# Local attention: doubled value tiles in three passes, another order of a turn, one mask for both halves

## The reference, cut to what matters

```python
# q: 16 heads, k and v: 2 heads of 64; blocks of 128 tokens, a band = the block before and the own block
kb, vb = band(k), band(v)
scores = einsum('bnqhgd,bnkhd->bnhgqk', qb, kb) * scale
diff = (BLOCK + arange(BLOCK))[:, None] - arange(2 * BLOCK)[None, :]
mask = ((diff >= 0) & (diff < WINDOW))[None] & kvalid[:, None, :]      # WINDOW = BLOCK = 128
scores = where(mask, scores, -inf)
probs = softmax(concatenate([scores, sink], -1))[..., :-1]
o = einsum('bnhgqk,bnkhd->bnqhgd', probs, vb)
y_sw = (o * silu(sw_z)) @ w_branch_swa
```

## Time and profile before

| | |
|---|---|
| median of 3 executions | 978.87 us (978.41 to 978.96) |
| profiled execution | 977.73 us |
| its span, first to last instruction | 975.9 us |
| mean granted PE clock | 0.998 |
| PE / DVE / ACT / POOL busy | 949.2 / 638.8 / 479.5 / 273.9 us |
| local attention, from PE's first score to the first product of slab 21 | 718.81 to 811.74 us |

### The profile page before, as it was taken

The page is one execution under the profiler, slowest core; times in us unless marked ns, Lnnn a source line. Parts: engine busy times, 40 slices in busy tenths (PEclk is TensorE's granted clock), DMA queues, the critical chain, the costliest instruction groups (busy, mean ns, idle before and its releaser), DMA issues.

```text
span 975.9 us, 12816 instructions
## 1 busy us (share of the span) xinstructions
PE 949.2 (97%) x4766; PEld 794.2 (81%) x4766; DVE 638.8 (65%) x921; ACT 479.5 (49%) x881; POOL 273.9 (28%) x208
## 2 busy tenths in 40 slices
PE   7999999999999999999999999998999889999997
PEld 6988888888888888888888888887887667888886
DVE  5677777937787687846666798699557775312214
ACT  5444655624435655725347777433556662222222
POOL 2216200003126200002342010430337996224231
PEclk9999999999999999999999999999999999999999
DMA  9332201232422301133233011131320112323312
GB/s 295 107 121 67 86 22 44 65 113 86 142 87 87 108 23 44 44 130 83 87 119 98 1 44 44 44 129 49 116 75 1 43 44 84 111 89 105 130 44 86
DMA packets 64990, 80.37 MB, mean 82 GB/s; under 512 B 5520, under 2 KB 48656, under 8 KB 64928
## 3 DMA queue, kind: packets, MB, share of 16 engines
q1 hardware_dynamic: 63024, 76.64, 24.5%
q10 hardware_dynamic: 1904, 2.88, 0.9%
HBM read 77.42 MB, written 2.10 MB: 81 GB/s over the span
## 4 chain that ended last, share of the span: by engine, by line
PE 43%; issue 31%; DVE 10%; POOL 9%; ACT 6%; DMA 1%; POOLq 0%; ACTq 0%; DVEq 0%
PE ps L1992 12%; PE ps L1993 11%; PE ps L1994 11%; POOL pwt L706 3%; PE ps L2051 1%; PE ps L2049 1%; PE ps L2050 1%; POOL yw L683 1%; POOL qw L691 1%; DVE rot L1848 1%; DVE wlo L1649 1%; DVE sp L1743 1%; ACT spr L1008 1%; POOL wlo L698 1%; DVE yw L1910 1%
## 5 line engine op out<-in xcount | busy, mean ns | idle before, releaser
L633 POOL TENSOR_TENSOR wlo<-raw,whi 128x2048 fp32r<-128x2048 f32 (+1 forms) x22 | 96.5, 4387 | 185.3 <-ACT whi L1002 175.9
L1992 PE MATMUL ps<-whi,hhi 128*128 128x512 f32 (+1 forms) x320 | 115.7, 362 | 1.1 <-issue 0.3
L1992 PE MATMUL ps<-hhi,whi 128*128 128x512 f32 x288 | 113.7, 395 | 3.3 <-DVE ysb L1286 2.5
L1994 PE MATMUL ps<-whi,hlo 128*128 128x512 f32 (+1 forms) x320 | 114.5, 358 | 0.0
L1993 PE MATMUL ps<-wlo,hhi 128*128 128x512 f32 (+1 forms) x320 | 114.4, 358 | 0.0
L1994 PE MATMUL ps<-hhi,wlo 128*128 128x512 f32 x288 | 112.3, 390 | 0.0
L1993 PE MATMUL ps<-hlo,whi 128*128 128x512 f32 x288 | 112.2, 390 | 0.0
L1002 ACT ACTIVATE whi<-raw 128x2048 fp32r<-128x2048 f32 (+1 forms) x29 | 52.9, 1826 | 81.7 <-PE ps L1994 73.2
L1320 DVE TENSOR_TENSOR wlo<-raw,whi 128x2048 fp32r<-128x2048 f32 (+1 forms) x29 | 63.6, 2192 | 37.4 <-ACT whi L769 30.9
L769 ACT ACTIVATE whi<-raw 128x2048 fp32r<-128x2048 f32 (+1 forms) x29 | 52.1, 1797 | 69.3 <-PE ps L1994 69.3
L2049 PE MATMUL ps<-hhi,whi 128*128 128x512 f32 x192 | 76.8, 400 | 0.0
(11 more groups left out here) (337 smaller groups left out, 2293.3 us busy)
## 6 DMA issues: line engine op xcount, KB each, us to landing
raw<-in_w_in SPq DMA_DIRECT2D x42, 1024.0 KB, 5.3
raw<-in_w_out SPq DMA_DIRECT2D x12, 1024.0 KB, 5.0
raw<-in_w_in SPq DMA_DIRECT2D x10, 512.0 KB, 3.9
raw<-in_w_branch_swa SPq DMA_DIRECT2D x4, 1024.0 KB, 5.0
raw<-in_w_branch_sb SPq DMA_DIRECT2D x4, 512.0 KB, 3.4
x<-in_x ACTq DMA_DIRECT2D x3, 512.0 KB, 6.7
out<-x SPq DMA_DIRECT2D x3, 512.0 KB, 2.6
ws<-in_spatial_w SPq DMA_DIRECT2D x2, 512.0 KB, 6.5
```

Of the source, the lines that this page charges most:

```text
L633: pool.tensor_tensor(wlo[s][:, 0:n, :], raw[s][:, 0:n, :], whi[s][:, 0:n, :].bitcast(F32), ALU.subtract).then_inc(slab_split, 1)
L1992: pe.matmul(out_ap, lhsT=lhi(k), rhs=rhi(k), start=first and k == 0, stop=False, skip_group_check=True)
L1994: m = pe.matmul(out_ap, lhsT=llo(k), rhs=rhi(k), start=False, stop=last and k == n - 1, skip_group_check=True)
```

## The change

- The value tiles are doubled instead of halved: `before_hi`, `before_lo`, `step_hi`, `step_lo` hold each half of a value twice (64 + 64 columns), so a product puts the same sum into both halves of the partitions. `window_values` runs three passes for the earlier values and three for the differences: six products instead of four. The 0.5 that stood in the tiles moves to the output.
- ACT makes the high halves of the differences ahead of the second half of the q tokens, and those of the earlier values after the last gate columns. POOL makes all low halves, and `v_step` itself behind slab 12's low half instead of slab 10's. DVE makes none.
- `other_half` and `window_gated` go. DVE's `window_out` takes PSUM times 0.5 times the gate at once.
- `window_own_low` goes. DVE masks both halves in one instruction, after a wait for its own split.
- Order of a turn: PE transposes turn w ahead of the values of turn w - 1, and the two gate steps of turn 0 come ahead of its transposes. DVE, ACT and POOL make a turn's maximum, exponentials, reciprocal and scaling one turn earlier; the outputs follow one turn after their products instead of two or three.
- Slab 18's low half goes from DVE to POOL, behind the first two scalings. Slab pieces keep their turns, counted from a loop shifted by one.

```diff
-                if j == 10:
+                if j == 12:
                     pool.wait_ge(tokw_copied, 3)
...
+            def values_low(lo, v, hi, copy_):
+                return pool.tensor_tensor(lo[:, :, :, copy_, :], v.rearrange("p t (g d) -> p t g d", g=2),
+                                          hi[:, :, :, copy_, :].bitcast(F32), ALU.subtract)
+            pool.wait_ge(vw_hi, 1)
+            for copy_ in range(2):
+                values_low(step_lo, v_step[:], step_hi, copy_).then_inc(vw_lo, 1)
+            pool.wait_ge(vw_hi, 2)
+            pool.wait_ge(tw_done, 10)
+            for copy_ in range(2):
+                values_low(before_lo[:, 0:1], insert_dim(v_meta[:], 1, 1), before_hi[:, 0:1], copy_)
+                values_low(before_lo[:, 1:], tokw[:, 0:3, 1152:1280], before_hi[:, 1:], copy_).then_inc(vw_lo, 1)
...
+            window_normalised(0)
+            window_normalised(1)
+            split2_lo(18)
             for w in range(16):
                 if w:
-                    window_own_low(w - 1)
-                if w >= 2:
-                    window_gated(w - 2)
-                if w >= 3:
-                    window_out_lo(w - 3)
+                    window_out_lo(w - 1)
+                if w < 14:
+                    window_normalised(w + 2)
...
+            def values_high(hi, v):
+                for copy_ in range(2):
+                    last = copy(hi[:, :, :, copy_, :], v.rearrange("p t (g d) -> p t g d", g=2))
+                return last
             for half in range(2):
                 split2(11 + 2 * half)
-                if half == 0:
+                if half == 1:
                     act.wait_ge(v_step_ready, 2)
+                    values_high(step_hi, v_step[:]).then_inc(vw_hi, 1)
...
             act.wait_ge(rope2_done, 5)
+            act.wait_ge(vw_lo, 2)
+            values_high(before_hi[:, 0:1], insert_dim(v_meta[:], 1, 1))
+            values_high(before_hi[:, 1:], tokw[:, 0:3, 1152:1280]).then_inc(vw_hi, 1)
...
+            merge_tanh(0)
+            for w in range(16):
+                transposed_hi(w)
+                if w == 14:
+                    split2(21)
+                if w < 14:
+                    window_exp(w + 2)
...
                 if w:
-                    other_half(w - 1)
+                    window_out_hi(w - 1)
...
                 low(pwt[:, 1, 0, :], ps[:, 4 + w % 2, :], pwt[:, 0, 0, :]).then_inc(tw_lo, 1)
-                dve.tensor_tensor(by_head(pwt[:, 0, 1, :]), by_head(pwt[:, 0, 0, :].bitcast(F32)),
-                                  insert_dim(own_keys.bitcast(F32), 1, 4), ALU.mult).then_inc(window_own_hi, 1)
+                dve.wait_ge(tw_lo, 10 + w + 1)
+                both = lambda own: pwt[:, :, own, :].rearrange("p s (h n) -> p s h n", n=P)
+                dve.tensor_tensor(both(1), both(0).bitcast(F32),
+                                  insert_dim(insert_dim(own_keys.bitcast(F32), 1, 4), 1, 2), ALU.mult).then_inc(window_own, 1)
...
-                    last = dve.tensor_tensor(yw[r, w % 2], o, other_part[r, w % 2], ALU.add)
+                    last = dve.scalar_tensor_tensor(yw[r, w % 2], o, 0.5, gate_sw[r, 2 * u:2 * u + 2, n * P:n * P + P],
+                                                    ALU.mult, ALU.mult)
...
+            window_norm(0)
+            window_norm(1)
+            window_max(2)
+            for w in range(16):
+                if w:
+                    window_out(w - 1)
+                transposed_lo(w)
+                if w == 14:
+                    slab2_low(21)
+                if w < 13:
+                    window_max(w + 3)
+                if w < 14:
+                    window_norm(w + 2)
+            window_out(15)
...
+                pe.wait_ge(tw_hi, 10 + w + 1)
+                pe.wait_ge(vw_lo, 4)
                 if w:
                     pe.wait_ge(swo_read, w)
+                v = lambda tile: tile[:, n, g].rearrange("p a d -> p (a d)")
+                pe.matmul(ps[:, 6, :], lhsT=v(before_hi), rhs=pwt[:, 0, 0, :], start=True, stop=False)
+                pe.matmul(ps[:, 6, :], lhsT=v(before_lo), rhs=pwt[:, 0, 0, :], start=False, stop=False)
+                pe.wait_ge(tw_lo, 10 + w + 1)
+                pe.matmul(ps[:, 6, :], lhsT=v(before_hi), rhs=pwt[:, 1, 0, :], start=False, stop=False)
+                pe.wait_ge(window_own, w + 1)
+                pe.matmul(ps[:, 6, :], lhsT=v(step_hi), rhs=pwt[:, 0, 1, :], start=False, stop=False)
+                pe.matmul(ps[:, 6, :], lhsT=v(step_lo), rhs=pwt[:, 0, 1, :], start=False, stop=False)
+                pe.matmul(ps[:, 6, :], lhsT=v(step_hi), rhs=pwt[:, 1, 1, :], start=False, stop=True).then_inc(swo_done, 1)
...
+                if w < 16:
+                    window_transposed(w)
                 if w:
                     window_values(w - 1)
-                if w < 16:
-                    window_transposed(w)
```

More of the change, by code:

```diff
@@ L700, in part_low, with window_normalised @@
                     ins.then_inc(slab_split, 1)
[L702 to L709, removed]
+            def window_normalised(w):
                 p4 = four_heads(pw, w)[:, :, 0:P]
@@ L1826, in stick_out @@
                 dve.wait_ge(ysb_ready, c + 1)
-            dve.wait_ge(vw_hi, 1)
-            for g in range(2):
-                d = slice(1152 + 64 * g, 1216 + 64 * g)
-                low(vwm[96:P, g, 64:128], v_meta[96:P, 64 * g:64 * g + 64], vwm[96:P, g, 0:64], 0.5)
-                low(vw[:, :, g, 64:128], tokw[:, :, d], vw[:, :, g, 0:64], 0.5)
-            def value_steps_low():
-                dve.wait_ge(vw_hi, 2)
-                for g in range(2):
-                    last = low(vd[:, :, g, 64:128], v_step[:, :, 64 * g:64 * g + 64], vd[:, :, g, 0:64], 0.5)
-                last.then_inc(vw_lo, 1)
             def rotate(v, cs, sn, rows, sem_):
@@ L1865, in _ @@
                         stick_out(t)
-                    if (half, t) == (0, 1):
-                        value_steps_low()
             dve.sem_inc(rope2_done, 5)
@@ L2530, in window_values @@
                 g = u // 2
-                pe.wait_ge(tw_lo, 10 + w + 1)
-                pe.wait_ge(vw_lo, 1)
+                pe.wait_ge(tw_hi, 10 + w + 1)
+                pe.wait_ge(vw_lo, 4)
                 if w:
                     pe.wait_ge(swo_read, w)
-                o = ps[:, 6, :]
-                before, change = vw[:, n - 1, g, :] if n else vwm[:, g, :], vd[:, n, g, :]
-                for part in range(2):
-                    pe.matmul(o, lhsT=before, rhs=pwt[:, part, 0, :], start=part == 0, stop=False)
-                pe.wait_ge(window_own_hi, w + 1)
-                pe.matmul(o, lhsT=change, rhs=pwt[:, 0, 1, :], start=False, stop=False)
-                pe.wait_ge(window_own_lo, w + 1)
-                pe.matmul(o, lhsT=change, rhs=pwt[:, 1, 1, :], start=False, stop=True).then_inc(swo_done, 1)
+                v = lambda tile: tile[:, n, g].rearrange("p a d -> p (a d)")
[7 more added lines that the diff above has]
+                pe.matmul(ps[:, 6, :], lhsT=v(step_hi), rhs=pwt[:, 1, 1, :], start=False, stop=True).then_inc(swo_done, 1)
             def merge_gate(i, k):
@@ L2567, in _ @@
                     window_scores(w + 2)
-                if 0 < w < 15:
-                    for n in range(GATE_STEPS[w - 1], GATE_STEPS[w]):
+                if w < 15:
+                    for n in range(GATE_STEPS[w - 1] if w else 0, GATE_STEPS[w]):
                         merge_gate(n // KT + 1, n % KT)
@@ L2575, in _ @@
                     stick_branch(20, w - 15).then_inc(unit_done, 1)
+                if w < 16:
+                    window_transposed(w)
                 if w:
                     window_values(w - 1)
-                if w < 16:
-                    window_transposed(w)
-                if w == 0:
-                    for n in range(GATE_STEPS[0]):
-                        merge_gate(1, n)
             slab2_here(21)
```

97 lines of the change are left out of this document (28 added, 69 removed).

## The result

The changed kernel takes **969.67 us** (median of 4 runs, 969.35 to 969.74) against 978.91 (4 runs, 978.41 to 979.35) for the kernel before on the same chip: ratio 0.9905, 95% interval 0.9888 to 0.9922. Its profiled execution took 969.72, with a span of 967.9. Of the 26 executions of the kernel before that were timed beside the experiments, 7 took 977.6 to 977.9 us at a mean granted TensorE clock of 0.998 to 0.999 and 19 took 978.7 to 981.0 at 0.996 to 0.997, while the profiled one (977.73) had 0.998 and the changed kernel's four had 0.998 to 0.999.

The account below looks back on a forecast made before the run. TensorE, 97% busy, bounds the kernel, idling in local attention on a ring through POOL. Gains of 5.3 there and 2.0 ahead of it take 977.73 to 970.4; 1.14 from profiled execution to median gives 971.6 us, range 966.5 to 977.0.

Parts of the forecast that it names:

- The ring through POOL: Local attention: each turn passes through POOL's mask, gating and subtraction and DVE's add and split; the change should unbind it.
- the stage: Local attention, 92.93 us before: 82.7 of PE work plus waits and restarts, 87.6 predicted, 5.3 less.
- PE's waits for the mask: Local attention: PE waits at the value products of turns 5, 12, 13 and 15, 2.2 us together.
- slab 19's last quarter: Local attention, gate step 24: PE waits 2.06 us because POOL reaches this subtraction only after scaling the ninth turn's weights.
- the restarts: Local attention: PE's restarts after its waits add 0.6 us.
- PE's own work: Local attention: scores, gate steps, transposes, value and branch products of the changed kernel add up to 82.7 us.
- The mask: Local attention: DVE's doubled 1024-column instruction takes 1.22 us, between 0.68 and 2.4, near 1.9 beside POOL.
- Rival (d): Local attention: the doubled mask costs 2.26 to 2.4 and DVE becomes the bound; 988 us, chance 0.08.
- rival (c): Local attention: the new output instruction also waits for POOL, 0.7 to 1.0 in most turns; 976.9 us, chance 0.12.
- Rival (a): Local attention: PE never waits, as DVE and POOL interleave better than written out; 967.3 us, chance 0.12.
- The third pass: Local attention: six value products a turn instead of four cost PE 7.3 us.
- The front: Ahead of the local attention: value lows leaving DVE shorten PE's 2.51 us wait at 670.49 by 2.0, between 0 and 2.5.

Follow-up runs that it names:

- e7: The changed kernel with PE's old order: values ahead of the transposes, turn 0's gate steps behind its transposes; 969.06 us.
- e5: The changed kernel with POOL's slab-quarter subtraction issued ahead of the scaling of the weights instead of behind it; 966.52 us.
- e3: The changed kernel without the products of the low value tiles, four value products a turn instead of six; 968.00 us.
- e1: The kernel before with the low halves of all value tiles moved to POOL; tiles, ring and order as before; 975.64 us.
- e2: The kernel before with both halves masked by one DVE instruction and POOL's mask gone, gating still on POOL; 971.48 us.
- e9: The kernel before with two edits, value tiles' low halves on POOL and the whole mask on DVE; 968.13 us.
- e8: The changed kernel with DVE's mask as two 512-column instructions, the first without the wait for the low half's split; 973.19 us.

## Why the prediction was right

**The mechanism held.** The ring through POOL is gone, DVE took the mask, and the stage came to 87.41 for 87.6 predicted. The four places of PE's waits for the mask (turns 5, 12, 13, 15) and the one for slab 19's last quarter are those that the turns, written out, had given. That the length of the stage came out within 0.2 is in part luck, as the next point shows.

**Two sizes were off against each other.** By the starts of PE's products in the changed kernel the mask's waits cost 1.6 and slab 19's quarter 1.8, where 2.2 and 2.06 were predicted, and the restarts 0.5 for 0.6: together 0.9 less. PE's own work is then 87.41 - 3.9 = 83.5 for the 82.7 that were added up: 0.8 more. The term that was too low is the value products, 23.4 for 22.0, of which 1.3 is the first product of a turn behind the transposes (e7); the scores were 0.9 too high, as they no longer stand behind the transposes.

**The prices.** The mask: 1.22 taken between 0.68 and 2.4, and 1.22 measured free; with POOL 1.59 to 1.96 where I had written "near 1.9". Rival (d) needed a mean of about 1.75; the mean is 1.52, so DVE missed being the bound by some 0.2 a turn. The output instruction keeps its price next to POOL, so rival (c) is false. Rival (a), no wait of PE in the stage, needed DVE and POOL to interleave better; e5 makes them do that by one move in POOL's order, and arrives at 966.5 where (a) said 967.3.

**The third pass.** I charged PE 7.3 us for it, which was right as work; e3 shows that taking it away gives 1.1, or about 2.7 without the fall of the clock, as PE would wait for DVE and POOL instead. The sum wasn't wrong, since it went by PE's content plus waits, but the sentence "the third pass costs 7.3" is, read as a price.

**The front** was mis-sized: 2.0 taken between 0 and 2.5, and 2.46 measured (e1: 2.77 at the start of the stage). The term that was mis-sized is what the third wait for a POOL slab and the alternation with the v_step subtractions take back of DVE's time. The alternation is there (654.14 and 655.29: 1.12 and 0.83 for the usual 0.43 and 0.69) but costs only 0.8, and DVE is done 0.17 us before PE needs its output at 668.02, so that the whole of PE's wait went, where 0.5 was to remain. The third wait itself took less than before (4.33 for an instruction of 0.69, against 5.08 for a pair of 0.76), as DVE came to it later.

**The time**: 971.6 predicted, 969.67 measured. Of the 1.9 us, 0.2 is the stage and 0.5 the front. The other 1.2 is the step from the profiled execution to the median: before, the profiled one lay 1.2 below its median, and I gave the changed kernel the same, but its profiled execution (969.72) lies at its median. That term was mis-sized: it is nothing here. What it stood for is probably the clock: the median of the kernel before lies among its executions at 0.997, e2's trace (0.997 as well) shows what the wait at slab 13 can cost in such an execution (1.2 us), and the changed kernel has neither that wait nor an execution below 0.998. So the median gained some 1.2 us that the prediction had no mechanism for. There is no trace of the kernel before at 0.997, and e1, without that wait, still has executions at 0.997, so where the clock falls in those is open.

## What to carry to other kernels

Where four engines pass a turn round, write the turn out for each engine with durations of its rows and look which ring closes last; moving one instruction out of the ring can be worth more than all rebuilding beside it (e2 and e9 against the whole change). Then look at the order on the engine that shares a port with the critical one: an instruction that isn't urgent, moved by one place so that it meets an instruction with a PSUM operand, gave 3.3 us here for no work at all. Work given to an engine that waits anyway is cheap until the wait is used up: here 7.3 us of products for 1.1, or 2.7 at an equal clock. And look at PE's clock behind each long wait before putting a difference down to the wait alone: in e3 and e8 1.6 us of it were the clock.

## What the runs showed of the hardware that was not expected

A row's length holds the time for which an instruction is kept off the port: POOL's 128x256 subtraction takes 0.74 to 2.79, the 1024-column mask 1.22 to 1.96, and DVE's pair of 128x64 rotations 0.36 to 4.64. Busy time so holds waits that no bracket shows; the shortest row of a form is its price. And cutting one DVE instruction into two of half its length made the pair longer (2.29 and 2.68, where the one mask takes 1.68 and 1.94 in the same turns of the changed kernel), since POOL is let in between; here the longer instruction was the cheaper one where the two engines compete.

TensorE's clock fell to its lower level behind a wait of 2.30 us (e3), 2.50 (e2) and 2.53 (e8), and cost 1.2 to 1.6 us each time; it stayed up behind 1.64 (the changed kernel), and behind 2.51 in the profiled execution of the kernel before. So a wait of this length can cost more than itself, and not in every execution.
